# Group 1's activated quarters made before group 0's block sums, and high weights first in the mixers' first unit

## The reference

```python
for l in range(DEPTH):                        # 2 layers
    (ssm_z, ssm_xbc, ...) = split_columns(h @ w_in[l])
    ...                                       # four mixers: ssm, mla, retention, nsa
    mix = jnp.concatenate([y_a, y_b, y_c, y_d], axis=-1) @ w_out[l]
    h = layer_norm(DEEPNORM_ALPHA * h + mix, ln1_g[l], ln1_b[l])
    ff = jnp.square(jax.nn.relu(h @ w_mlp1[l])) @ w_mlp2[l]
    h = layer_norm(DEEPNORM_ALPHA * h + ff, ln2_g[l], ln2_b[l])
```

## Time and profile before

| | |
|---|---|
| median of three executions | 2842.62 us |
| the profiled execution, its own time | 2847.2 us |
| its span | 2845.4 us |
| TensorE busy | 2720.9 us (96%), 13986 matmuls |
| VectorE busy | 1790.9 us (63%) |
| ScalarE busy | 1136.3 us (40%) |
| mean granted clock of TensorE | 0.977 of full speed |

### The profile page before, as it was taken

One profiled execution on the slowest core, in us unless ns is written; L12 is line 12 of the kernel. 1 busy time (PEld: TensorE's weight loads), 2 busy tenths in 40 slices (PEclk: granted clock), 3 DMA queues, 4 the chain that ended last, 5 costly groups with the idle time before them and its releaser, 6 DMA issues. The chain is left out here.

```text
span 2845.4 us, 37143 instructions
## 1 busy us (share of the span) xinstructions
PE 2720.9 (96%) x13986; PEld 2183.4 (77%) x13986; DVE 1790.9 (63%) x2939; ACT 1136.3 (40%) x1817; POOL 252.0 (9%) x220
## 2 busy tenths in 40 slices
PE   5999989999989999999999999899999899999997
PEld 5899866656868887888888998566568688878886
DVE  5654554454787776776856444535547877758778
ACT  3322223334355554433433222234343555543343
POOL 3121222000000000000011112220000000000000
PEclk9999989999999999999999999799999999999998
DMA  4223234102315445997621233421032354479875
GB/s 164 71 68 94 91 92 92 31 1 82 103 64 176 143 144 192 384 312 247 225 86 38 77 100 97 101 54 30 1 119 89 97 163 145 141 261 364 290 230 188
DMA packets 254360, 387.29 MB, mean 136 GB/s; under 512 B 38608, under 2 KB 126800, under 8 KB 254184
## 3 DMA queue, kind: packets, MB, share of 16 engines
q1 hardware_dynamic: 254184, 384.92, 42.3%
HBM read 288.05 MB, written 96.83 MB: 135 GB/s over the span
## 5 line engine op out<-in xcount | busy, mean ns | idle before, releaser
L2747 ACT ACTIVATE att_PT<-att_ST 128x512 f32<-128x512 f32 (+2 forms) x244 | 135.3, 554 | 327.3 <-PE att_ST L2639 196.0
L1626 PE MATMUL mix_acc<-mix_whi,x_hi 128*128 128x256 f32 (+1 forms) x640 | 185.5, 290 | 0.0
L998 PE MATMUL dense_tr<-mlp_w,mlp_a 128*128 128x512 f32 x448 | 175.9, 393 | 6.3 <-DVE mlp_w L1302 6.3
L1628 PE MATMUL mix_acc<-mix_whi,x_lo 128*128 128x256 f32 (+1 forms) x640 | 180.1, 281 | 0.0
L1627 PE MATMUL mix_acc<-mix_wlo,x_hi 128*128 128x256 f32 (+1 forms) x640 | 180.0, 281 | 0.0
L1000 PE MATMUL dense_tr<-mlp_w,mlp_a 128*128 128x512 f32 x448 | 174.9, 390 | 0.0
L999 PE MATMUL dense_tr<-mlp_w,mlp_a 128*128 128x512 f32 x448 | 174.9, 390 | 0.0
L998 PE MATMUL dense_acc<-mlp_w,mlp_a 128*128 128x512 f32 x448 | 174.4, 389 | 0.0
L999 PE MATMUL dense_acc<-mlp_w,mlp_a 128*128 128x512 f32 x448 | 174.4, 389 | 0.0
L1000 PE MATMUL dense_acc<-mlp_w,mlp_a 128*128 128x512 f32 x448 | 174.4, 389 | 0.0
L644 POOL TENSOR_TENSOR norm_rstd<-norm_var,norm_power 128x1 f32<-128x1 f32 x32 | 29.8, 932 | 1474.1 <-DVE norm_var L624 1474.1
(11 more groups left out here) (432 smaller groups left out, 7461.1 us busy)
## 6 DMA issues: line engine op xcount, KB each, us to landing
mlp_w_raw<-w_mlp SPq DMA_DIRECT2D x124, 512.0 KB, 6.1
blocks<-h SPq DMA_DIRECT2D x32, 1792.0 KB, 8.4
mlp_a_raw<-blocks SPq DMA_DIRECT2D x72, 512.0 KB, 4.5
mlp_raw<-w_mlp SPq DMA_DIRECT2D x66, 512.0 KB, 6.1
ahead<-w_in SPq DMA_DIRECT2D x20, 1024.0 KB, 6.6
mlp_temp<-blocks SPq DMA_DIRECT2D x38, 512.0 KB, 4.9
residual<-h SPq DMA_DIRECT2D x32, 512.0 KB, 3.9
h<-residual SPq DMA_DIRECT2D x32, 512.0 KB, 9.7
```

Source lines behind the costliest of these rows:

```text
L998: pe.matmul(out, ah, wh, start=(ch == 0 and k == 0), stop=False, skip_group_check=True)
L1626: pe.matmul(out, xh, whi[b][:, k, 0:n], start=(k == 0), stop=False)
L1628: mm = pe.matmul(out, xl, whi[b][:, k, 0:n], start=False, stop=(k == KT - 1))
L2747: act.activation(PT[0:width, n % 3, c0:512], ST[0:width, n % 2, c0:512], ACT.Exp).then_inc(s.exp_ready, 1)
```

## The change

1. Quarters 12 and 21 of group g get places in the group's own stage: where `block_sums(g)` will later write product 7's and product 6's left factors. The wait for the block sums of the group before goes. In its place there is one for the store of two groups ago (`blocks_stored`), which freed that stage.
2. `block_sums` takes its five sums in the order 2, 5, 1, 6, 7, and the last two, which overwrite the quarters, wait until those that read them are done (`quarter_read`).
3. For group 1, ScalarE's `activate` goes one position earlier, from (2, 2) to (1, 7). VectorE forms group 1's quarters at (1, 7) and group 0's block sums at (2, 2), where it was the other way round.
4. The mixers' first unit does the two passes of a pair of rows that need only high weights as soon as the high half is there, and the pass with low weights one pair later.

```diff
+        a12_of, a21_of = (lambda g: stage[g % 2][:, 6, :]), (lambda g: stage[g % 2][:, 5, :])
...
                 def activate(g, i):
                     act.wait_ge(s.multiplied, at[g, i] + 1)
-                    if g:
-                        act.wait_ge(s.blocks_ready, g)
+                    if g >= 2:
+                        act.wait_ge(blocks_stored[g % 2], 16 * (g // 2))
                     else:
+                        act.wait_ge(s.z_turned, NT)
...
                         elif i == 2:
                             if g == 2:
-                                activate(1, 4)
-                                activate(1, 3)
                                 square(1, 6)
                             square(g - 1, 7)
...
                     elif (g, i) == (1, 7):
                         square(0, 7)
+                        activate(1, 4)
+                        activate(1, 3)
...
-                    for i in (1, 2, 5, 6, 7):
+                    for n, i in enumerate((2, 5, 1, 6, 7)):
                         (a, b), op = PRODUCTS[i].left
+                        if i in (6, 7):
+                            dve.wait_ge(s.quarter_read, 2 * g + n - 2)
                         mm = dve.tensor_tensor(stage[g % 2][:, i - 1, :], part[a], part[b], op)
+                        if i in (2, 5):
+                            mm.then_inc(s.quarter_read, 1)
...
                         elif (g, i) == (2, 2):
-                            rests(1)
-                            quarter22(1)
-                            quarter11(1)
-                    elif (g, i) == (0, 1):
-                        rests(0)
-                    elif (g, i) == (1, 7):
-                        block_sums(0)
+                            block_sums(0)
+                    elif (g, i) in ((0, 1), (1, 7)):
+                        gather(g)
+                        rest12(g)
+                        rest21(g)
+                        rest1(g)
+                        if g:
+                            quarter22(g)
                     if i == 6 and g != 1:
                         quarter22(g)
-                    elif i == 7 and g != 1:
+                    elif i == 7:
                         quarter11(g)
...
+                    if unit == 0:
+                        for part in range(5):
+                            if part < 4:
+                                pe.wait_ge(s.first_hi, part + 1)
+                                for k in (2 * part, 2 * part + 1):
+                                    pe.matmul(out, whi[b][:, k, cols], hi[:, k, half * 512:(half + 1) * 512], start=(k == 0), stop=False)
+                                    pe.matmul(out, whi[b][:, k, cols], lo[:, k, half * 512:(half + 1) * 512], start=False, stop=False)
+                            if part:
+                                pe.wait_ge(s.first_lo, part)
+                                for k in (2 * part - 2, 2 * part - 1):
+                                    mm = pe.matmul(out, wlo[b][:, k, cols], hi[:, k, half * 512:(half + 1) * 512], start=False, stop=(k == KT - 1))
+                        mm.then_inc(s.unit_done, 1)
+                        return
                     for k in range(KT):
-                        if unit == 0 and k % 2 == 0:
-                            pe.wait_ge(s.first_lo, k // 2 + 1)
```

More of the change, by code:

```diff
@@ L482, in dense @@
         stage = [flat[:, 7 * 512 * b:7 * 512 * (b + 1)].rearrange("p (i n) -> p i n", i=7) for b in range(2)]
-        a12, a21 = flat[:, 14 * 512:15 * 512], flat[:, 15 * 512:16 * 512]
+        a12_of, a21_of = (lambda g: stage[g % 2][:, 6, :]), (lambda g: stage[g % 2][:, 5, :])
         z_tile = lambda t: h[:, t % 3, :]
@@ L1074, in activate @@
                 def activate(g, i):
-                    dst, bank, relu, ready = (a12, tr[:, g % 2, :], s.relu12, s.ready12) if i == 4 else (a21, acc[:, g % 2, :], s.relu21, s.ready21)
+                    dst, bank, relu, ready = (a12_of(g), tr[:, g % 2, :], s.relu12, s.ready12) if i == 4 else (a21_of(g), acc[:, g % 2, :], s.relu21, s.ready21)
                     act.wait_ge(s.multiplied, at[g, i] + 1)
-                    if g:
-                        act.wait_ge(s.blocks_ready, g)
+                    if g >= 2:
+                        act.wait_ge(blocks_stored[g % 2], 16 * (g // 2))
                     else:
+                        act.wait_ge(s.z_turned, NT)
                         act.wait_ge(s.sum_ready, sum_at[7, HT - 1] + 1)
@@ L1231, in block_sums @@
                 def block_sums(g):
-                    part = {(0, 0): stage[g % 2][:, 2, :], (1, 1): stage[g % 2][:, 3, :], (0, 1): a12, (1, 0): a21}
+                    part = {(0, 0): stage[g % 2][:, 2, :], (1, 1): stage[g % 2][:, 3, :], (0, 1): a12_of(g), (1, 0): a21_of(g)}
                     dve.wait_ge(s.ready22, 2 * g + 2)
```

## The result

The changed kernel is slower: 2851.11 us (median of 8 runs, 2848.11 to 2853.70) against 2842.31 us (8 runs, 2840.18 to 2843.82). The ratio is 1.0033 [1.0023, 1.0042], which is +9.4 us [6.5, 11.9]. The forecast was +9.8 us and 2852.4 us.

What follows compares the result with a forecast made beforehand. The start of (2,7) was taken as the bound, set by group 3's weights loading behind group 0's store. 9.8 (that start) + 1.5 (clock) - 1.5 (mixers) = +9.8 us on 2842.62: 2852.4 us, range 2846.5 to 2856.5.

Steps and rivals of the forecast that it cites:

- The chain: MLP: late load of group 3's weights starts product (2,7) 4.9 us later a layer, 9.8 us in all.
- Rival (b): MLP: shortening the gap at (2,3) is what pays; 9.4 to 12.3 us faster, about 2832 us; chance 0.07.
- Rival (a): MLP: group 3's load comes at about today's time, leaving the mixers' 1.5 us: 2841 us; 0.11 with other no-change ways.
- The clock: MLP, around (2,7): low clock behind the new gap loses 1.5 us, in one layer of two; ends 0 and 3.
- rival (c): MLP: low clock after both gaps in both layers, no mixers' gain: 12.8 us slower, 2855.4 us; counted within the forecast's 0.82.
- The mixers: Mixers' first unit: TensorE starts 0.75 us earlier a layer, 1.5 us gained in all; ends 0 and 3.
- The sum: Whole kernel: 9.8 + 1.5 - 1.5 = +9.8 us, giving 2852.4 us.
- Rival (d): MLP steady part: the wait for stores of two groups ago holds ScalarE's activations, each of 14 groups paying; 1 in 100.

Runs made afterwards that it cites:

- e4: Changed kernel with group 3's load issued ahead of group 0's store, as soon as group 1's weights are split: 2836.21 us, ratio 0.9981.
- e6: Changed kernel with group 3's load issued when group 0's block sums are done, but ahead of group 0's store: 2847.40 us, ratio 1.0013.
- e3: Kernel before with only group 3's load issued ahead of group 0's store, once group 1's weights are split: 2843.61 us, ratio 1.0000.
- e7: e4 with group 2's quarters 12 and 21 at their old places, so ScalarE needs no store there: 2830.25 us, ratio 0.9949.
- e1: Kernel before with only the new order of passes in the mixers' first unit: 2843.58 us, ratio 1.0000.
- e9: e1 run again, the mixers' part alone on the kernel before: 2842.89 us, ratio 0.9993.
- e2: Changed kernel with the old mixers' first unit, so the MLP's part alone: 2857.53 us, ratio 1.0047.
- e5: Kernel before with the new quarter places, store wait and order inside block sums, but the old order of work: 2841.64 us, ratio 0.9992.
- e8: e7 with ScalarE's copies of (2,2) and (2,5) moved ahead and group 1's block sums one position later: 2824.86 us, ratio 0.9935.
- e11: e8 run again, the same kernel: 2823.77 us, ratio 0.9931.
- e10: e8 with the mixers' first unit as in the kernel before: 2826.63 us, ratio 0.9939.

## Why the prediction was right, step by step

*The chain.* Right, with its sizes, for the changed kernel. The step that carries the forecast is that the start of (2,7) is set by group 3's weights, behind a store that waits for the block sums. The block sums came 5.40 us later (forecast 5.55), the load was used 5.33 us later (5.55), (2,7) started 4.69 us later (4.9), each in the scale above. e4 and e6 change nothing but this load's place in the queue, and the wait at (2,6) goes with it: 7.76 and 7.82 us in the changed kernel, 3.40 and 4.66 in e6, none in e4. For the kernel before the prediction was too strong: that the start of (2,7) "isn't set by the 6.74 us gap" holds in the second layer only, by e3.

*The gap was not the price by itself.* The stretch against before, in us a layer: the change, which shortens the gap and puts the load back, +6.3 and +6.4; the load moved alone (e3) +0.1 and -1.2; both (e4) -1.2 and -0.9; both with the store wait away (e7) -6.0. So shortening the gap pays once the chain behind it is cut. A shorter gap with the load left at its time was not run; that it would give nothing is argued from the copy at 865.65. Rival (b) fell as its condition said: the weights would have had to come 4 us earlier, and they came 5.33 later. The Trainium skill's advice (Perfetto Trace Analysis, section Optimization Strategy) to find the semaphore behind each gap and let it come sooner was not borne out by the change, where the copy of product 5 came sooner and the kernel got slower, and was in e7.

*Rival (a), the load isn't late.* Fell by the row at 857.40: 10.5 us from issue to use, as before (10.6). In e6, with the store behind it, the same transfer takes 6.6 and 7.8 us. The Trainium skill has 6.15 us for 1 MB (DMA: Bandwidth & Descriptors, section Bandwidth), as the busy time of a transfer issued from GpSimd. The times here run from the issue on SyncE to the use: the 5.6 us of the earlier trace rows and the 6.6 of e6 are near that figure, the 10.5 behind a store of 1.75 MB are not.

*A gap that was missed.* I had TensorE wait at (2,3) alone, 2.8 us. It waited 1.18 us for the copy of (2,2) and 1.16 for that of (2,5), 2.3 in all: the copy of (2,2) stands behind the four activations that were moved. Behind gaps this short the clock stayed at 1.00, where before it fell behind the 6.74 us, so (2,1) was done earlier and TensorE then waited 7.76 us and not the 6 forecast for the same event. It costs nothing, as it isn't the end of the chain.

*The clock.* Mis-sized. I took a loss of 1.5 us in one of the two layers at (2,7); it came in both (gaps of 1.95 and 2.15 us), as rival (c) had it for this place. The other half of (c), no gain in the mixers, did not show in the traces, and its 12.8 us lie above the interval of the measured time.

*The mixers.* Mis-sized on the other side if the traces are right, 2.9 us between the two traces (3.0 in the mean of all) and not 1.5. I left the clock out of the forecast's own value and had it in the range: the wait fell from 2.76 to 2.03 us and the low clock sometimes didn't come.

*The sum.* 12.7 from the two stretches less 3.0 is +9.7 us, measured +9.4. The forecast was 9.8 + 1.5 - 1.5: the missed 1.5 of the clock in the second layer and the extra gain in the mixers cancel, so the closeness to 0.4 us is in part luck. The same ledger (both stretches' difference to before, less 3.0 with the new mixers) lies inside the timed interval of every other kernel but e1, where it is 0.6 us outside:

| kernel | ledger, us | timed, us |
|---|---|---|
| e1, e9 | -3.2, -3.0 | 0.0, -2.0 |
| e2 | +12.8 | +13.4 |
| e3 | -1.1 | 0.0 |
| e4 | -5.1 | -5.4 |
| e5 | -0.4 | -2.3 |
| e6 | +4.1 | +3.7 |
| e7 | -15.0 | -14.5 |
| e8, e11 | -19.5, -19.7 | -18.5, -19.6 |
| e10 | -16.7 | -17.3 |

*Rival (d).* Not in the steady part, where TensorE has no wait. But its mechanism is there once, at group 2, below the load's wait. The prediction had it done in time, which holds as long as the load is late. In e4 it is the next wait: its expectation had it at 5.5 us and missed by 2.6 us or more, since the store took 6.9 and (2,7) came 2.0 us later than expected.

**What stays open.** Why the clock falls behind some gaps of 1.8 to 2.3 us and not behind others, and how much of the mixers' gain reaches the time. The ledger leaves one such place out. At (0,4), ahead of the stretch, TensorE waits 1.84 to 1.91 us in every trace. Behind that gap the clock fell in both layers of the kernel before, and (0,5) started 8.55 and 8.54 us after (0,4). In the changed kernel it fell in neither layer, and these were 6.98 and 6.94 us:

```profile
795.04 0.47 PE L979 MATMUL dense_tr<-x_hi,mlp_ring_low 128*128 128x512 f32 x1 [1.91 <-ACT mlp_copy L1063]
...
796.00:799.00 3.00, 3.00 (x19) 2.53 (x19) 1.95 (x4) 0.68 (x2) 0.00 (x0) 1.00 0.43 175
```

So these two traces differ there by 3.2 us, which no term of the sum has. Over all traces the clock fell in 8 of 10 such starts with the old mixers and in 7 of 16 with the new; that is too few to say whether the change has a part in it.

## What to carry to other kernels

Before a gap is shortened, follow the next product that waits, or that would wait if it came earlier: if another chain ends at the same time, the gap may be only cover for it. And when work is put ahead of a step, look at what that step releases on an in-order DMA queue: here 3 us of vector work put back held a load behind a store, and cost more than the shorter gap gave. Then move the load, and look for the wait that lay hidden below it, before judging the idea: the same change, with the load ahead and two tiles at places of their own, is 14.5 us faster than before and not 9.4 slower.

## What the runs showed of the hardware

A load of 1 MB and a store of 1.75 MB issued 0.4 us apart share the DMA engines. From the first issue to the use of the second the pair takes 10.9 us with the store first (changed) and 11.5 and 12.3 with the load first (e6, first and second layer):

```profile
848.00:856.00 8.00, 2.99 (x14) 2.13 (x12) 0.00 (x0) 0.00 (x0) 0.00 (x0) 0.96 1.04 317
```

This is the changed kernel while both run: the DMA engines are busy all the time (share 1.04) and move 317 GB/s. Which of the two comes first decides when each is done. The load takes 6.6 and 7.8 us ahead of the store (e6), 10.5 and 10.6 behind it; the store takes 6.9 us with no load near it (e4) and 11.0 and 11.9 behind one (e6).

The granted clock stayed at 1.00 behind all gaps of 1.15 to 1.63 us in this part of the MLP and was 0.50 behind those of 1.89 us and more at (2,7). Elsewhere both were seen. At (0,1) it fell behind 1.93 us in 25 of 26 starts, at (0,4) behind 1.84 to 1.91 us in 15 of 26. At the mixers' start, behind 2.03 and 2.29 us, it differs in the same kernel: e8 and e11 have 68.21 and 69.83 us there in the first layer, with the same wait of 2.03 us.
